# Squared-relu layers: the first product of 28 of 32 feature tiles by seven half-size products

## What is computed

```python
def sq_relu_mlp(h, w1, w2):            # h: 512 x 1024, w1: 1024 x 4096, w2: 4096 x 1024
    u = jax.nn.relu(h @ w1)
    return (u * u) @ w2
# per layer
x = x + sq_relu_mlp(rmsnorm_2(x, norm_mlp[layer]), w_mlp1[layer], w_mlp2[layer])
```

## Time and profile before

| | |
|---|---|
| median of 3 runs | 2446.11 us (2445.96 to 2446.32) |
| the profiled execution: span of its instructions | 2446.3 us |
| what lies around the span in the profiled execution | none can be seen: the span is as long as the longest of the three runs |
| mean granted clock of TensorE | 0.993 |
| busy: PE, PEld, DVE, ACT, POOL | 98%, 78%, 50%, 39%, 8% |
| DMA | 208.50 MB, mean 85 GB/s |

### The profile page before, as it was taken

The page is one execution under the profiler, slowest core; times in us unless marked ns, Lnnn a source line. Parts: engine busy times, 40 slices in busy tenths (PEclk is TensorE's granted clock), DMA queues, the critical chain, the costliest instruction groups (busy, mean ns, idle before and its releaser), DMA issues.

```text
span 2446.3 us, 28445 instructions
## 1 busy us (share of the span) xinstructions
PE 2390.1 (98%) x11206; PEld 1912.1 (78%) x11206; DVE 1234.3 (50%) x2012; ACT 962.0 (39%) x1613; POOL 196.0 (8%) x147
## 2 busy tenths in 40 slices
PE   8999999999999999999999999999999899999998
PEld 7888888777777788888887677888887677888887
DVE  5533436788654445433336855424435775532432
ACT  4323224455432334322323554313324785431432
POOL 0100100322102000100100200000001100000000
PEclk9999999999999999999999999999999999999999
DMA  4323323211222232323323113322232012333332
GB/s 144 104 87 103 98 88 102 77 52 52 70 69 72 63 108 81 101 80 110 95 83 99 59 53 103 104 94 95 95 96 64 29 46 80 97 101 95 95 95 70
DMA packets 66805, 208.50 MB, mean 85 GB/s; under 512 B 7408, under 2 KB 15856, under 8 KB 66416
## 3 DMA queue, kind: packets, MB, share of 16 engines
q1 hardware_dynamic: 66672, 206.68, 27.1%
HBM read 204.55 MB, written 2.10 MB: 84 GB/s over the span
## 4 chain that ended last, share of the span: by engine, by line
PE 90%; DVE 4%; ACT 3%; issue 2%; DMA 1%; POOL 0%; POOLq 0%; SPq 0%; ACTq 0%; DVEq 0%
PE bank L1842 26%; PE bank L1846 26%; PE bank L1844 26%; PE bank L2009 2%; PE bank L1971 1%; PE bank L2016 1%; PE bank L2000 1%; PE bank L2062 1%; ACT whi L2130 1%; PE bank L1917 1%; DVE wlo L2435 1%; PE bank L1913 1%; PE bank L1915 1%; DMA wraw<-in_stream 1%; PE bank L1936 1%
## 5 line engine op out<-in xcount | busy, mean ns | idle before, releaser
L2435 DVE TENSOR_TENSOR wlo<-wraw,whi 128x1024 fp32r<-128x1024 f32 (+5 forms) x436 | 487.9, 1122 | 541.9 <-ACT whi L2130 541.1
L1842 PE MATMUL bank<-hhi,whi 128*128 128x512 f32 x1736 | 693.2, 399 | 11.4 <-ACT whi L2130 9.4
L1846 PE MATMUL bank<-hhi,wlo 128*128 128x512 f32 x1736 | 681.7, 393 | 2.1 <-DVE wlo L2435 2.1
L1844 PE MATMUL bank<-hlo,whi 128*128 128x512 f32 x1736 | 680.7, 392 | 0.4 <-DVE hlo L2442 0.4
L2130 ACT ACTIVATE whi<-wraw 128x1024 fp32r<-128x1024 f32 (+5 forms) x436 | 408.9, 940 | 493.2 <-PE bank L1846 425.0
L1842 PEld LDWEIGHTS bank<-hhi,whi 128*128 128x128 f32 x1736 | 328.1, 189 | 84.2 <-ACT whi L2130 11.4
L1846 PEld LDWEIGHTS bank<-hhi,wlo 128*128 128x128 f32 x1736 | 327.7, 189 | 74.9 <-DVE wlo L2435 5.1
L1844 PEld LDWEIGHTS bank<-hlo,whi 128*128 128x128 f32 x1736 | 328.2, 189 | 67.3 <-DVE hlo L2442 2.2
L1844 PE MATMUL bank<-mlo,whi 128*128 128x512 f32 x576 | 227.8, 395 | 0.2 <-DVE mlo L2742 0.2
L1842 PE MATMUL bank<-mhi,whi 128*128 128x512 f32 x576 | 227.8, 396 | 0.0
L1846 PE MATMUL bank<-mhi,wlo 128*128 128x512 f32 x576 | 227.7, 395 | 0.0
(11 more groups left out here) (419 smaller groups left out, 3094.7 us busy)
## 6 DMA issues: line engine op xcount, KB each, us to landing
wraw<-in_stream SPq DMA_DIRECT2D x343, 512.0 KB, 3.5
wraw<-in_stream SPq DMA_DIRECT2D x32, 192.0 KB, 2.4
wraw<-in_stream SPq DMA_DIRECT2D x22, 256.0 KB, 2.6
wraw<-in_stream SPq DMA_DIRECT2D x26, 128.0 KB, 2.0
wraw<-in_stream SPq DMA_DIRECT2D x8, 320.0 KB, 2.9
xa<-in_x SPq DMA_DIRECT2D x8, 256.0 KB, 6.4
out<-ya SPq DMA_DIRECT2D x8, 256.0 KB, 2.7
m<-in_mask SPq DMA_DIRECT2D x1, 1024.0 KB, 4.8
```

Of the source, the lines that this page charges most:

```text
L1842: pe.matmul(out, sh, xh, start=first, stop=False)
L1844: pe.matmul(out, sh, xl, start=False, stop=False)
L1846: p = pe.matmul(out, sl, xh, start=False, stop=end and last)
L2435: dve.tensor_tensor(wlo[j][:, 0:L], wraw[i][:, 0:L], whi[j][:, 0:L].bitcast(f32), SUB).then_inc(*lo.up(c))
```

## The change

Of each layer's 32 feature tiles the first four stay. The other 28 go in seven groups of four. A group's product is a 2x2 block product: weights in four quarters (two feature tiles by four k slices, A), activations in four quarters (four k slices by 256 tokens, B). Instead of eight quarter products there are seven, of 24 matmuls of 256 columns each. Their weights are quarters and sums of quarters, their activations quarters and four sums of quarters.

- **Weight sums.** SP fetches the four quarters of a group (512 KB each). The sums come about in the fetched buffer itself: POOL issues a DMA that reads another quarter again from HBM and accumulates it onto the buffer (four per group: for q7, p5, p6 and q3). q7, p6 and q3 reuse the buffer of q1, so that POOL waits for wlo of q1, q7 and p6 before it. Every product has a chunk of its own: seven splits where there were four.
- **Raw buffers.** In these layers there are six for fetched weights in place of two. mhi and mlo shrink to eight slices, so a layer now goes in four parts (two groups each, the first one group and the four plain tiles), and the second product is summed into ya in four pieces of eight features.
- **Activation sums.** At the layer's start POOL multiplies the eight slices of ya by the norm's gain into xa (`plain`) and forms the four sums (`token_sum`, 128x1024 each). ACT and DVE split them into hi and lo (`token_parts`).
- **Results.** ACT copies q1's bank out before q2 accumulates on it (`first_copy`). DVE forms two shared sums V and W (`shared`) and the four corners of the group, each followed by relu, square and the two parts (`corner`: relu and combination on DVE, square and mhi on ACT, mlo on DVE).
- **Second product.** In each part the first halves (k slices 0 to 3) of the first two output tiles run before the others, over features of the part's first group.

In the diff "up" and "low" stand for pairs of quarters; the order of the products is that of `PRODUCTS`.

```diff
+PRODUCTS = (("q1", 0, None, None), ("q7", 0, 1, "q1"), ("p5", 1, 2, None), ("p6", 0, 2, "q7"), ("q2", 3, None, None),
+            ("q4", 2, None, None), ("q3", 0, 3, "p6"))
+NARROW, WIDE = 2, 6
...
+    def seven(tag, blk, s, quarters):
+        at = len(raws)
+        for pair in quarters:
+            raws.append(Raw(pair, s))
+        index = {}
+        for name, raw, plus, settled in PRODUCTS:
+            index[name] = len(plan)
+            plan.append(Chunk((tag, blk, name), at + raw, 8, 128, None if plus is None else at + plus,
+                              None if settled is None else index[settled]))
+        for raw, name in ((0, "q3"), (1, "p5"), (2, "q4"), (3, "q3")):
+            raws[at + raw].gone = index[name]
...
     def mlp(l):
-        for half in range(2):
-            for f in range(16):
-                col(f"m{l}u{half}", f"mlp1_{l}", half * 16 + f)
+        s, mat = 4 + 2 * l, f"mlp1_{l}"
+        for part in range(4):
+            for b in range(2):
+                f = 8 * part + 4 * b
+                if f == 0:
+                    for n in range(4):
+                        col(f"m{l}u", mat, n)
+                else:
+                    seven(f"m{l}s", f, s, rows_and_cols([mat] * 4, (f + 2, f + 3, f, f + 1)))
             for n in range(8):
-                col(f"m{l}d{half}", f"mlp2_{l}", n, 16, half * 16)
+                add((f"m{l}d{part}", n, 0), f"mlp2_{l}", part * 8, 8, n * 128, 128, s)
...
         def square(t, f):
             q = T.take()
...
+        def seven(f):
+            bank, last = {}, {}
+            over = {"q2": "q1", "q4": "q7", "q3": "p5"}
+            for name, *_ in PRODUCTS:
+                c = opened((f"m{l}s", f, name))
+                if name in over:
+                    b, was = bank[over[name]], (last[over[name]],)
+                else:
+                    b = G.take()
+                    was = b.was
+                bank[name] = b
+                put("seven", s, name, c, b.i, was, name not in over)
+                closed.add(c)
+                done = ("used", c)
+                key = (s, f)
+                if name == "q1":
+                    put("first_copy", key, b.i, V.i, (done, *V.free))
+                    last["q1"] = ("first_copy", key)
+                elif name == "p6":
+                    put("shared", key, b.i, bank["q7"].i, V.i, W.i, (done, *W.free))
+                    b.free = (("combined", ("v", key)),)
+                    last["q7"] = ("combined", ("w", key))
+                    q = T.take()
+                    put("corner", key, "c22", bank["p5"].i, W.i, q.i, ("combined", ("w", key)), q.was, afree)
+                    last["p5"] = W.free = ("combined", (key, "c22"))
+                    W.free = (W.free,)
+                    q.free = (("v_lo", (key, "c22")),)
+                elif name in over:
+                    part = {"q2": "c11", "q4": "c21", "q3": "c12"}[name]
+                    q = T.take()
+                    put("corner", key, part, b.i, V.i, q.i, done, q.was, afree)
+                    q.free = (("v_lo", (key, part)),)
+                    b.free = (("relu" if part == "c11" else "combined", (key, part)),)
+                    if name == "q3":
+                        V.free = (("combined", (key, part)),)
+            return ("used", c)
+        for part in range(4):
+            if part == 0:
+                ts = side_by_side(("h", s), *[(f"m{l}u", n, 0) for n in range(3)])
+                paid = open_sums[R.next].tok
+                for j in range(8):
+                    put("plain", s, j, (*x_at[j], *paid))
+                    if j == 3:
...
+                for n in (3, 2, 4):
+                    put("token_sum", s, n, ())
+                ts.append(run(feat([(f"m{l}u", 3, 0)], ("h", s))))
                 R.step()
                 for f, t in enumerate(ts):
                     square(t, f)
-                f = 4
-            while f < 16:
-                t = run(feat([(f"m{l}u{half}", half * 16 + f, 0)], ("h", s)))
-                square(t, half * 16 + f)
-                f += 1
-            h_end = t.end
-            x = ("v", s, half * 16)
-            if half == 0:
+                for n in (3, 1, 2, 4):
+                    put("token_parts", s, n, guard)
+                h_end = seven(4)
+            else:
+                seven(8 * part)
+                h_end = seven(8 * part + 4)
+            x = ("v", s, 8 * part)
+            begun = [feat([(f"m{l}d{part}", n, 0)], x) for n in range(2)]
+            for tile in begun:
+                next(tile)
+            if part < 3:
                 for n in range(8):
-                    t = run(feat([(f"m{l}d0", n, k0) for k0, _ in groups(16)], x))
-                    put("resid", ("mlp", s), n, t.bank, (t.end, *x_at[n]))
-                    t.freed(("x_dve", (("mlp", s), n)))
...
+                elif k == "seven":
+                    s, name, c, b, was, fresh = a
+                    _, _, i = chunk(c)
+                    w.wait_ge(*hi[c])
+                    waits(was)
+                    for n in range(8):
+                        xh, xl, ev_h, ev_l = quarter_of(s, name, n % 4)
+                        out = banks[b][:, 256 * (n // 4):256 * (n // 4) + 256]
+                        sh, sl = whi[i][:, n * 128:n * 128 + 128], wlo[i][:, n * 128:n * 128 + 128]
+                        w.wait_ge(*ev_h)
+                        pe.matmul(out, sh, xh, start=fresh and n == 0, stop=False, skip_group_check=True)
+                        w.wait_ge(*ev_l)
+                        pe.matmul(out, sh, xl, start=False, stop=False, skip_group_check=True)
+                        w.wait_ge(*lo[c])
+                        p = pe.matmul(out, sl, xh, start=False, stop=n == 7, skip_group_check=True)
+                    p.then_inc(*used.up(c))
...
                     c, = a
-                    L, i, j = chunk(c)
-                    w.wait_ge(s_raw[i], 16 * (c // NR + 1))
+                    L, src, j = chunk(c)
+                    if plan[c].plus is None:
+                        w.wait_ge(*landed(plan[c].raw))
+                    else:
+                        w.wait_ge(*summed[c])
                     if c >= NW:
                         w.wait_ge(*used[c - NW])
-                    act.activation(whi[j][:, 0:L], wraw[i][:, 0:L], F.Copy).then_inc(*hi.up(c))
+                    act.activation(whi[j][:, 0:L], src[:, 0:L], F.Copy).then_inc(*hi.up(c))
...
+                elif k == "shared":
+                    key, b6, b7, v, u, after = a
+                    w.wait_ge(*first_copy[key])
+                    waits(after)
+                    dve.tensor_tensor(ftmps[:, v, :], banks[b6][:, :], ftmps[:, v, :], SUB).then_inc(*combined.up(("v", key)))
+                    w.wait_ge(*combined["v", key])
+                    dve.tensor_tensor(ftmps[:, u, :], banks[b7][:, :], ftmps[:, v, :], ADD).then_inc(*combined.up(("w", key)))
+                elif k == "corner":
+                    (s, f), part, b, v, q, after, was, afree = a
+                    key = ((s, f), part)
+                    vhi, vlo, p = corner_of(s, f, part)
+                    scale = rb[:, p].rearrange("q (a b) -> q a b", a=1).to_broadcast([128, 2, 256])
+                    tq = tmps[:, q, :]
+                    w.wait_ge(*rbm["h", s])
+                    w.wait_ge(*at(after))
+                    waits(was)
+                    if part == "c11":
+                        dve.scalar_tensor_tensor(two(tq), two(banks[b][:, :]), 0.0, scale, MAX, MUL).then_inc(*relu.up(key))
+                    else:
+                        if part == "c22":
+                            p = dve.tensor_tensor(tq, ftmps[:, v, :], banks[b][:, :], SUB)
+                        elif part == "c21":
+                            p = dve.tensor_tensor(tq, ftmps[:, v, :], banks[b][:, :], ADD)
+                        else:
+                            p = dve.tensor_tensor(tq, banks[b][:, :], ftmps[:, v, :], SUB)
+                        p.then_inc(*combined.up(key))
+                        w.wait_ge(*combined[key])
+                        dve.scalar_tensor_tensor(two(tq), two(tq), 0.0, scale, MAX, MUL).then_inc(*relu.up(key))
+                    w.wait_ge(*v_hi[key])
+                    dve.tensor_tensor(vlo, two(tq), vhi.bitcast(f32), SUB).then_inc(*v_lo.up(key))
...
+                elif k == "split":
+                    c, = a
+                    ch = plan[c]
+                    if ch.plus is None:
+                        continue
+                    w.wait_ge(*landed(ch.raw))
+                    if ch.settled is not None:
+                        w.wait_ge(*lo[ch.settled])
+                    pool.dma_start(raw_at(ch.raw)[:, :], in_stream(ch.plus), accum_op=ADD).then_inc(summed[c][0], 16)
+                elif k == "plain":
+                    s, j, after = a
+                    waits(after)
+                    w.wait_ge(*before.now())
```

(54 more changed lines are left out.)

149 lines of the change are left out of this document (105 added, 44 removed).

## The result

The changed kernel takes 2612.01 us, median of 4 runs (2608.84 to 2617.55); the kernel before, 4 runs, 2446.03. The ratio is 1.0686, 95% interval 1.0671 to 1.0701. The forecast was 2604 in a range of 2535 to 2700. The profiled execution has a span of 2609.0 us and a mean granted clock of 0.965 (0.993 before).

A forecast was written before the change was run, and what follows sets the result against it. The prediction took PE's issue time to bound the kernel, with splits running ahead. Pairs +79, layer starts +68 and clock +11 gave +158 on 2446.3, so 2604 us, in a range of 2535 to 2700.

The forecast's parts named there:

- PE's own work: On PE, a group goes from 21.76 to 20.16 us, 1.60 gained; fourteen groups give -22.4 us if nothing waits.
- L: Time from POOL's issue of an accumulating DMA to its landing; taken as 6 us, bounds 3.5 and 7.8.
- loop of one corner and one split: On ACT and DVE, a corner with combination and its split cost 4.15 + 0.79 = 4.94 us.
- The pair: Two groups in a row, T = 0 at the first q1: waits 16.3 us, 13.1 after gains; six pairs +79.
- waits of 2 to 6 us for wlo: Sign expected in the profile: such PE waits in the second group of each pair, none in the first.
- The formula 4.3 + 2L: PE's wait per pair of groups, at the second product's seventh slice; 16.3 us with L at 6.
- The clock: TensorE's clock falls after waits: 1.4 us for each pair and layer's start, 8 x 1.4 = +11, bounds 0 and 30.
- The first group of a layer: At a squared-relu layer's start, p5's late accumulation delays squares and token sums: +34 us each, two layers +68.
- POOL's arithmetic: Eight products and four sums on POOL before p5's accumulation: 16.8 us, bounds 10.6 and 21.8, to 1514.7.
- rival of slow accumulations: Accumulating DMAs much slower, L about 10, sharing engines with SP's loads: 2734 us; chance 17%.
- that of a start without a stall: At a layer's start POOL finishes early, by the tiles' end; only pairs and their clock cost: 2533 us; chance 6%.
- that of the splits staying ahead: ACT and DVE keep ahead, accumulations land in under about 2 us, PE never waits: 2424 us; chance 5%.

The follow-up runs named there:

- experiment 7: Against the kernel before: part 0 all plain tiles, each later part one seven-product group followed by four plain tiles, 6 groups in all; 2436.27 us, ratio 0.9959.
- experiment 3: The changed kernel with POOL's 56 accumulating DMAs as plain loads of the same bytes; 2585.44 us, ratio 1.0561 against the kernel before.
- experiment 2: The changed kernel without its 56 accumulating DMAs, each split waiting for the fetched quarter alone; 2510.39 us, ratio 1.0255 against the kernel before.
- experiment 4: The changed kernel with the split of the next group's q1 moved ahead of corner c22 on ACT and DVE; 2581.53 us, ratio 1.0545 against the kernel before.
- experiments 1: The changed kernel with POOL issuing p5's accumulation ahead of its twelve arithmetic operations at each layer's start; 2583.01 us, ratio 1.0551 against the kernel before.

## Why the prediction came out right

**PE's own work** was right: 256-column matmuls lie 0.12 apart, and experiment 7 shows 1.8 us per group where it took 1.60.

**L**, taken as 6 with bounds 3.5 and 7.8: the landing took 5.4 us. ScalarE's timeline and POOL's in the pair after 1611.75:

```profile
1635.72 1.06 ACT L2325 ACTIVATE whi<-wraw 128x1024 fp32r<-128x1024 f32 x1 [4.00 <-DMA wraw<-in_stream]
...
1640.59 1.04 ACT L2325 ACTIVATE whi<-wraw 128x1024 fp32r<-128x1024 f32 x1
...
1645.45 1.04 ACT L2325 ACTIVATE whi<-wraw 128x1024 fp32r<-128x1024 f32 x1
...
1653.34 1.06 ACT L2325 ACTIVATE whi<-wraw 128x1024 fp32r<-128x1024 f32 x1 [4.47 <-DMA wraw<-in_stream]
```

```profile
1630.33 1.75 POOL L3157 DMA_DIRECT2D wraw<-in_stream  x2 [14.85 <-DVE wlo L2648]
...
1648.04 0.86 POOL L3157 DMA_DIRECT2D wraw<-in_stream  x1 [8.86 <-DVE wlo L2648]
```

From issue to split it is 1635.72 - 1630.33 = 5.4 and 1653.34 - 1648.04 = 5.3. The two splits between them lie 4.87 and 4.86 apart: the loop of one corner and one split, predicted as 4.94.

**The pair**, with T = 0 at 1611.75, went step by step as the prediction has it. PE starts on q7's wlo at T + 26.3 (20.3 + L; here and below with L = 6), q3's sum is issued at T + 36.3 and its split ends at T + 43.8 (32.4 + 2L = 44.4), q4' starts at T + 45.4 (46.0), the wait in the second product ends at T + 61.9 (63.6). The wait is then 61.9 - 47.3 = 14.6 where it took 16.3, net 11.4, and the clock behind it cost more, see below: 14.3 in all, where 13.1 + 1.4 stood. The sum for a pair is thus right to 0.2 us by some luck: a wait 1.7 too long and a clock term 1.5 too short cancel. Nor does the delay look as the prediction said it would, as waits of 2 to 6 us for wlo. TensorE's rows between T and T + 62 show 9.6 us of waits, the longest 2.10 for whi, 2.08 for the shared sums and 2.69 for mhi, those for wlo 0.24 to 0.76. The rest of the delay passes in slow matmuls (granted clock 0.87 from 1636.83 to 1662.89).

The formula 4.3 + 2L holds for plain loads too: at their 3.9 us it gives 8.9 over before and 1.4 for the clock, 10.3, and experiment 3 has 10.7. It fails without sums: there the pair's end hangs on PE's q4', so the wait has a floor. The formula gives 1.1 and the clock, 2.5 us over before, and experiment 2 has 4.7. An estimate from the two starts of V' puts the floor at L = 1.7 (5.4 less half of 7.4), below the prediction's lower bound of 3.5.

**The clock** is the term that was mis-sized in the pairs. The second product after the wait at 1673.67 ends 51.5 us after it began (1662.89 to 1714.39); it takes 44.8 undisturbed (192 matmuls) and stood 2.7, so 4.0 are the clock's. Of these 2.9 lie behind the wait and add to the part (162 matmuls in 40.7 us instead of 37.8); the others lie ahead of it, where the wait would have taken them anyway. The prediction had one fall of 1.4 us, seven matmuls. TensorE's timeline behind the wait:

```profile
1674.99 0.63 PE L2022 MATMUL bank<-mhi,wlo 128*128 128x512 f32 x1
...
1676.70 0.63 PE L2018 MATMUL bank<-mhi,whi 128*128 128x512 f32 x1
...
1680.09 0.39 PE L2018 MATMUL bank<-mhi,whi 128*128 128x512 f32 x1
...
1680.79 0.40 PE L2018 MATMUL bank<-mhi,whi 128*128 128x512 f32 x1
```

Four steps of 0.43 (1.2 GHz), and three of 0.233 (2.4 GHz) from 1680.09 on. The first two matmuls lie 0.73 and 0.59 apart, since mlo comes after mhi (DVE writes it from 1673.65 to 1674.34). In the second group of the change slow matmuls cost nothing of their own, as V' waits there for q3's split and not for PE.

**The first group of a layer** is the term most off: 34 + 1.4 predicted, 41.2 measured, and the step is POOL's arithmetic, 16.8 us (to 1514.7). POOL's timeline:

```profile
1497.20 1.01 POOL L3157 DMA_DIRECT2D wraw<-in_stream  x1 [86.55 <-DVE wlo L2648]
1497.97 1.87 POOL L3162 TENSOR_SCALAR xa<-ya,cols 128x512 f32<-128x512 f32 x1
1500.00 1.56 POOL L3162 TENSOR_SCALAR xa<-ya,cols 128x512 f32<-128x512 f32 x1 [0.17 <-POOL xa L3162]
...
1505.11 2.34 POOL L3168 TENSOR_TENSOR xa<-xa 128x1024 f32<-128x1024 f32 x1
...
1514.47 7.21 POOL L3168 TENSOR_TENSOR xa<-xa 128x1024 f32<-128x1024 f32 x3
1521.62 1.80 POOL L3157 DMA_DIRECT2D wraw<-in_stream  x2
```

It took 23.7 us (1497.97 to 1521.62). The sums were right (2.34 for 2.3). The multiplications take 1.56, the first 1.87, and with the step between them 1.73, where 0.8 was taken and 1.285 was the upper bound. All bounds for a one-input operation were below what it costs, and the whole lies above its upper bound of 21.8. From p5's landing on the prediction holds again: ACT's split is at 1527.09 and PE gets thi at 1540.37, 13.3 us later, as predicted (1520.7 to 1534.0). From there to the wait in the second product it is 31.4 us (to 1571.80), 33.4 predicted.

PE also stood still 6.9 us before 1510.12, for rcs, DVE's inverse root of the norm. The prediction left this out. DVE computes it behind q7's split, and that split waits for q7's own accumulation. ACT's splits of q7 and p5:

```profile
1502.63 1.06 ACT L2325 ACTIVATE whi<-wraw 128x1024 fp32r<-128x1024 f32 x1 [7.32 <-DMA wraw<-in_stream]
1527.09 1.06 ACT L2325 ACTIVATE whi<-wraw 128x1024 fp32r<-128x1024 f32 x1 [23.41 <-DMA wraw<-in_stream]
```

It changes nothing, since PE would have waited that long for thi anyway.

**Sum.** Predicted 79 + 68 + 11 = 158; measured 6 x 14.3 + 2 x 41.2 = 168, less the 4 us of the untouched stretch, and 166.0 between the medians. Pairs right, by two errors that cancel; starts 6 us too low each: 6.9 for POOL's arithmetic and 0.7 for the clock (behind the wait 39.95 us instead of 37.8), less 2.0 behind thi. The range took that in, though the term itself lay outside its bounds. The rival of slow accumulations (L about 10) falls with 5.4; that of a start without a stall falls with the 23.7 us of waiting for thi; that of the splits staying ahead holds only where plain tiles follow (experiment 7).

**Left open.** A start still costs 12.5 us more than before without sums and squares (87.7 for 75.2), and was not taken apart further: POOL's arithmetic and the order of the token parts remain in it. How much of the 4.8 us of experiment 4 is the clock was not separated. Why the matmuls of the second product lie 0.233 apart and those of the first 0.227, before and after alike, isn't explained by these runs.

## What to carry to other kernels

A saving on the bounding engine that adds work to the engines feeding it is worth only what their chain allows: add up the dependent steps between two of the bounding engine's blocks (here seven splits and four corners, 24.5 us by the prediction's terms, of which one corner and split, 4.94, measured 4.87) against the block's length (20.2), and if it is longer, put cover behind each block rather than two blocks in a row. Count every step that a queue executes in order, in front of the one that others wait for; here one such step on POOL was worth 29 us and one in ACT's and DVE's list 30. A transfer that may only begin when a buffer is read stands in the chain with its whole latency, and costs what other work doesn't cover (here 7.4 of 10.8 us for two), at a DMA share of only 0.48.

## What the runs showed that was not expected

- POOL takes 1.56 us for a 128x512 multiplication by a per-partition scalar (one input), longer than the 1.285 of two inputs of the same size.
- An accumulating DMA of 512 KB that POOL issues lands in 5.4 us, a plain one in 3.9, SP's in 3.4. One such instruction lasts 0.95 us on POOL on average (two in a row overlap, and all 56 keep it busy for 48.9 us), a plain one 0.54.
- A chain of dependent DVE operations of 128x512 advances by 0.72 per step in the change (V, W and the combination at 1623.38, 1624.11, 1624.83), 0.79 by the earlier trace rows.
- DVE is slowed at places where POOL computes. DVE's timeline of the change at the layer's start, and that of the kernel before for the same instruction of four elements:

```profile
1503.72 1.51 DVE L2648 TENSOR_TENSOR wlo<-wraw,whi 128x1024 fp32r<-128x1024 f32 x1 [7.16 <-ACT whi L2325]
...
1505.33 2.14 DVE L2624 TENSOR_SCALAR rcs<-sm 128x4 int32<-128x4 int32 x1
```

```profile
1498.37 0.17 DVE L2411 TENSOR_SCALAR rcs<-sm 128x4 int32<-128x4 int32 x1
```

  2.14 us for 0.17: it ends at 1507.47, with POOL's token sum (1505.11 + 2.34 = 1507.45). It is so again in the second layer (2.14 us) and in experiments 2 and 7 (2.20 and 2.21 at 1499.72 and 1499.26), each time up to the end of a token sum of POOL's; beside a multiplication the same instruction took 0.47 (experiments 1 and 3). A split's wlo took 1.51 for 1.22 beside a multiplication. No run here was made to find the reason.
